# Decoder layer with 32 experts on one core: order of the experts by token count, routing on the unnormalised residual, and a last block of its own

## The reference

```
x = LN(alpha*x + mixer(x));  x = LN(alpha*x + MemCrossAttn(x, mem))
logits = x @ router_w + router_b          # 32 experts
top_val, top_idx = top_k(logits, 4);  gate = softmax(top_val)
for each chosen expert e:  h = clamped_swiglu(x @ w_gate[e] + b_gate[e], x @ w_up[e] + b_up[e])
                           y += gate * (h @ w_down[e] + b_down[e])
x = LN(alpha*x + y)
```

## Time and profile before

| | us |
|---|---|
| median of 3 runs | 1252.56 (1250.12 to 1252.93) |
| time of the profiled execution | 1252.49 |
| span of the profiled execution | 1250.4 |
| TensorE busy | 1089.8 (87%), 7535 instructions |
| VectorE busy | 317.5 (25%) |
| ScalarE busy | 189.5 (15%) |
| GpSimd busy | 35.7 (3%) |
| moved | 446.56 MB, mean 357 GB/s |

### The profile page before, as it was taken

How to read it: one execution, slowest core, us unless ns; L and a number is a source line. 1 busy time by engine, 2 the same in 40 slices (tenths; PEclk the granted TensorE clock), 3 DMA queues, 4 the chain that set the end, 5 groups by cost and what they waited for, 6 DMA issues and landing times.

```text
span 1250.4 us, 19511 instructions
## 1 busy us (share of the span) xinstructions
PE 1089.8 (87%) x7535; PEld 493.7 (39%) x7536; DVE 317.5 (25%) x973; ACT 189.5 (15%) x433; POOL 35.7 (3%) x38
## 2 busy tenths in 40 slices
PE   8999999999899999999966789776699797967885
PEld 6777874965433333333312223222233232322321
DVE  1757433213322222222211122111122221211123
ACT  1231331121111111111100011100011111100111
POOL 0110010100100000000000000000000000000001
PEclk9999999999999999999988799878799898987988
DMA  9733140557899989999999999999999999999995
GB/s 363 275 138 135 68 157 20 202 221 301 347 429 429 429 345 403 408 401 409 428 428 429 429 428 429 430 429 428 428 428 428 428 429 428 429 430 429 428 428 234
DMA packets 43687, 446.56 MB, mean 357 GB/s; under 512 B 6912, under 2 KB 7376, under 8 KB 19088
## 3 DMA queue, kind: packets, MB, share of 16 engines
q1 hardware_dynamic: 39616, 442.43, 84.5%
q10 hardware_dynamic: 4048, 3.81, 1.0%
HBM read 445.18 MB, written 1.05 MB: 357 GB/s over the span
## 4 chain that ended last, share of the span: by engine, by line
PE 60%; DMA 25%; DVE 5%; issue 3%; another core or an unknown queue 2%; DVEq 2%; SPq 1%; POOL 0%; POOLq 0%; ACT 0%; ACTq 0%
DMA main<-in_exp_w_up_dram 24%; PE bank L1318 23%; PE bank L1359 10%; PE bank L882 8%; PE bank L872 6%; PE bank L1255 2%; PE bank L1346 2%; PE bank L1122 2%; DVEq L1807 1%; DVE kst L1813 1%; DVE main L1810 1%; DVE main L1800 1%; PE bank L931 1%; DMA main<-in_w_in_dram 1%
## 5 line engine op out<-in xcount | busy, mean ns | idle before, releaser
L1318 PE MATMUL bank<-main 128*32 128x512 f32 x3008 | 392.0, 676 | 122.2 <-DMA main<-in_exp_w_up_dram 117.7
L1318 PEld LDWEIGHTS bank<-main 128*32 128x32 f32 x3008 | 113.3, 122 | 393.8 <-issue 360.1
L1359 PE MATMUL bank<-main,kst 128*32 128x512 f32 x1504 | 180.8, 598 | 16.9 <-DVE kst L1813 16.9
L1800 DVE TENSOR_TENSOR main<-bank,main 128x256 f32<-128x256 f32 x94 | 39.6, 421 | 590.9 <-PE bank L1346 590.9
L882 PE MATMUL bank<-main 128*128 128x512 f32 x256 | 111.8, 593 | 0.3 <-ACT main L693 0.3
L815 ACT ACTIVATE main<-bank 128x512 f32<-128x512 f32 x47 | 28.1, 598 | 479.2 <-PE bank L1318 479.2
L1297 PE MATMUL bank<-main 64*128 64x512 f32 x384 | 95.4, 615 | 0.7 <-ACT main L823 0.7
L872 PE MATMUL bank<-main 128*128 128x256 f32 x352 | 77.8, 380 | 0.0
L1359 PEld LDWEIGHTS bank<-main,kst 128*32 128x32 f32 x1504 | 39.3, 109 | 90.1 <-issue 64.1
L882 PEld LDWEIGHTS bank<-main 128*128 128x128 f32 x256 | 48.2, 190 | 56.7 <-issue 56.5
L872 PEld LDWEIGHTS bank<-main 128*128 128x128 f32 x352 | 66.5, 190 | 10.1 <-issue 1.1
(11 more groups left out here) (252 smaller groups left out, 707.0 us busy)
## 6 DMA issues: line engine op xcount, KB each, us to landing
main<-in_exp_w_gate_dram SPq DMA_DIRECT2D x64, 2048.0 KB, 30.2
main<-in_exp_w_up_dram SPq DMA_DIRECT2D x64, 2048.0 KB, 34.7
main<-in_exp_w_down_dram SPq DMA_DIRECT2D x64, 2048.0 KB, 36.7
...
```

What stands on the lines that cost most here:

```text
L1318: last = pe.matmul(gu_bank[at:at + CAP, :], xg_chunk(k), weights(role, k, f), start=(k == 0), stop=(k == KC - 1))
L1359: last = pe.matmul(y_bank[at:at + CAP, :], hT[:, j, f, :], weights(role, j, h), start=(f == 0 and pair == 0), stop=(f == 1 and pair == 1))
L1800: return tt(dst, gT[:, :, w, :, :], b.unsqueeze(3).broadcast_to([P, 4, 2, CAP]), ALU.add)
```

## The change

1. **Order of the experts.** Experts 0 and 1 stay first. The other 30 are ranked by token count on the chip (VectorE compares keys of 64 x count minus the expert's number), and a fixed table (`rank_at_position`) takes lightest but one, heaviest, next lightest, next heaviest and so on; the very lightest comes last. SP reads the expert's number for a position from the table (one more `value_load` an expert), TensorE goes by positions. With the counts above the blocks by position are 1, 1, 1, 3, and then 1 and 2 in turn through position 29: positions 4 to 29 alternate 1 and 2, positions 30 and 31 have one block each.
2. **Router on the residual.** The router's weights are multiplied by the norm's gain ahead of time, and mean and bias are folded in (unit `rw`). TensorE transposes the raw residual and multiplies it; VectorE scales the logits by the reciprocal root (`choose`). `xa_wo` is loaded as two halves of columns, and the units run `wo0`, `wo2`, `wo1`, `wo3` with the transposes between. `keep_warm` is gone. Token block 1 is normalised by ScalarE, its gain and bias are applied half by GpSimd and half by VectorE, and the first gather waits for both (`ln_ready` 5). Two of the four products that begin the result sums (`begin_sum`) stand behind the first gather.
3. **Tables.** `bT` moves to the cross attention. The counts are taken twice, as a column and as a row; `block_counts` has five products and `block_table` two.
4. **First transfers.** G0 and U0 of expert 0 take the slots of `xa_wq`'s halves and are released after `xq3`; D0 of expert 1 is released with G1 and U1.
5. **Last block.** It has code of its own on TensorE, ScalarE and VectorE. The scatter of the block before and the gates' transposes stand between the two halves of gate and up; gather, selection and gathered transposes are left out. The last D1 transfer is two transfers, each with its own semaphore.
6. **Last norm.** ScalarE sums and squares token block 1 with its accumulator; VectorE does all the rest; GpSimd only computes the two roots.

The diff, cut to its core (drains and blank lines left out, indentation shortened):

```diff
+def rank_at_position():
+    heavy, light = list(range(FIRST_EXPERTS, 16)), list(range(16, N_EXPERTS))
+    last = light.pop()
+    order = list(range(FIRST_EXPERTS))
+    while heavy or light:
+if light:
+    order.append(light.pop())
+if heavy:
+    order.append(heavy.pop(0))
+    return np.array(order + [last])
...
+    tie = np.where(e < FIRST_EXPERTS, 1e6 * (FIRST_EXPERTS - e), 0.0) - e
+    out[:, K_RANK + R_KEY:K_RANK + R_KEY + N_EXPERTS] = tie
+    out[0:N_EXPERTS, K_RANK + R_KEYCOL] = tie
...
-ROLE_SLOT = [(N_ATT + r) % SLOTS for r in range(SLOTS)]
+ROLE_FOLLOWS = [13, 14, 11, 12, 15, 16]
+ROLE_RELEASES = [13, 13, 15, 15, 16, 17]
+ROLE_SLOT = [i % SLOTS for i in ROLE_FOLLOWS]
...
     sp.wait_ge(mix_ready, 4)
     load_role(G0, 1, odd=True)
+    load_first(G0)
+    load_first(U0)
     sp.wait_ge(unit_filled, UNIT_AT["xs3"] + 1)
     load_role(U0, 1, odd=True)
-    for role in (G0, U0, G1, U1):
-        load_first(role)
+    load_first(G1)
+    load_first(U1)
     sp.wait_ge(unit_filled, UNIT_AT["oT3"] + 1)
     load_role(G1, 1, odd=True)
     load_role(U1, 1, odd=True)
+    load_role(D0, 1, odd=True)
     load_first(D0)
     load_first(D1)
-    sp.wait_ge(unit_filled, UNIT_AT["router"] + 1)
-    load_role(D0, 1, odd=True)
-    sp.wait_ge(ln_ready, 4)
+    sp.wait_ge(ln_ready, 5)
     load_role(D1, 1, odd=True)
     sp.wait_ge(tab_ready, 1)
...
+    def load_last_down(e):
+        w = d["exp_w_down"][0].rearrange("e (h p i j) n -> e h p i (j n)", h=2, i=2, j=2)
+        at = weights_at(D1, True)
+        for i in range(2):
+            cols = slice(at + i * SLOT_COLS // 2, at + (i + 1) * SLOT_COLS // 2)
+            sp.dma_start(main[:, cols], w[bass.ds(e, 1), 1, :, i, :].rearrange("e p n -> p (e n)")).then_inc(last_down[i], 16)
...
+    def load_expert(p, ahead, odd, last=False):
+        done = blocks_through(p, ahead - 2)
+        e = sp.value_load(itab[0:1, bass.ds(p + (T_ORDER + ahead), 1)], min_val=0, max_val=N_EXPERTS - 1)
         sp.wait_ge(gu0_used, done)
-        load_role(G0, e, odd, ahead)
-        load_role(U0, e, odd, ahead)
...
+    load_expert(N_EXPERTS - 4, 2, odd=False)
+    load_expert(N_EXPERTS - 4, 3, odd=True, last=True)
...
+    pool.wait_ge(scaled_x, 1)
+    pool.tensor_tensor(x3[:, 1, 0:HALF], x3[:, 1, 0:HALF], ln_g[:, 0:HALF], ALU.mult)
+    pool.drain()
+    pool.tensor_tensor(x3[:, 1, 0:HALF], x3[:, 1, 0:HALF], ln_b[:, 0:HALF], ALU.add).then_inc(ln_ready, 1)
...
+    act.wait_ge(offset_in, 1)
+    for h in range(2):
+        part = x3[:, 1, h * HALF:(h + 1) * HALF]
+        act.activation(part, part, ACT.Identity, scale=rstd_fin[1], bias=offset).then_inc(scaled_x, 1)
...
+        act.wait_ge(scat_done, 3 + h)
+        act.activation(x3[:, 1, h * HALF:(h + 1) * HALF], acc[1][h][:, :], ACT.Copy,
+                       accum_out=sums_fin[:, h:h + 1]).then_inc(sum_done, 1)
+    act.wait_ge(mean_ready, 1)
+    for h in range(2):
+        act.activation(x3[:, 1, h * HALF:(h + 1) * HALF], acc[1][h][:, :], ACT.Square, bias=offset,
+                       accum_out=sums_fin[:, h:h + 1]).then_inc(square_done, 1)
...
-    for i in range(4):
-        if i == 3:
-            pe.wait_ge(ln_applied, 3)
-            tokens_T("x2T", 0, x3)
-            tokens_T("x2T", 1, x3)
-        token_major(f"wo{i}", oT, i // 2, through(15, 16), (i % 2) * HALF, ((0, "oT2"), (6, "oT3")))
...
-    def keep_warm(products):
...
+    arrived(15)
+    ps = begin("wo0")
+    need("oT2")
+    wo_steps(ps, 0, range(0, 6))
+    need("oT3")
+    wo_steps(ps, 0, range(6, 8)).then_inc(unit_filled, 1)
+    wo_steps(begin("wo2"), 2, range(0, 8)).then_inc(unit_filled, 1)
+    need("wo0")
+    tokens_T("x2T", 0, x3)
+    used_up(1, "wo2")
+    arrived(16)
+    wo_steps(begin("wo1"), 1, range(0, 8)).then_inc(unit_filled, 1)
+    need("wo2")
     tokens_T("x2T", 2, x3)
+    bank_wo3 = begin("wo3")
+    wo_steps(bank_wo3, 3, range(0, 4))
+    need("wo1")
+    tokens_T("x2T", 1, x3)
+    wo_steps(bank_wo3, 3, range(4, 8)).then_inc(unit_filled, 1)
+    def route(ps, b, steps):
+        for k in steps:
+            last = pe.matmul(ps[:, 0:N_EXPERTS], x2T[b][:, k, :], router_w3[:, k, :], start=(k == 0), stop=(k == KC - 1))
+        return last
+    def begin_sum(i):
+        pe.matmul(begin(f"acc{i}")[:, :], alpha_eye, x3[:, i // 2, (i % 2) * HALF:(i % 2 + 1) * HALF],
+                  start=True, stop=False).then_inc(unit_filled, 1)
+    need("rw", "x2T1")
+    route(begin("rt0"), 0, range(0, 8)).then_inc(unit_filled, 1)
+    used_up(1, "wo3")
+    need("wo3")
     tokens_T("x2T", 3, x3)
-    keep_warm(6)
-    route_block(1, ((0, "x2T2"), (4, "x2T3"))).then_inc(unit_filled, 1)
+    ps = begin("rt1")
+    need("x2T2")
+    route(ps, 1, range(0, 4))
+    pe.wait_ge(x2T3_first, 1)
+    route(ps, 1, range(4, 6))
+    need("x2T3")
+    route(ps, 1, range(6, 8)).then_inc(unit_filled, 1)
     pe.wait_ge(alpha_ready, 1)
-    for i in range(4):
-        ps = warm_bank if i == 0 else begin(f"acc{i}")
-        pe.wait_ge(ln_ready, 3 if i < 2 else 4)
-        pe.matmul(ps[:, :], alpha_eye, x3[:, i // 2, (i % 2) * HALF:(i % 2 + 1) * HALF],
-                  start=True, stop=False).then_inc(unit_filled, 1)
-    pe.wait_ge(route_ready, 1)
+    pe.wait_ge(ln_ready, 3)
+    begin_sum(0)
+    pe.wait_ge(chosen, 1)
     ps = begin("pos")
     pe.matmul(ps[:, 0:32], strict, M[:, 0:32], start=True, stop=True)
-    pe.matmul(ps[:, 32:64], strict, M[:, 32:64], start=True, stop=False)
-    pe.matmul(ps[:, 32:64], ones, M[:, 0:32], start=False, stop=True)
+    pe.matmul(ps[:, 32:64], ones, M[:, 0:32], start=True, stop=False)
+    pe.wait_ge(chosen, 2)
+    pe.matmul(ps[:, 32:64], strict, M[:, 32:64], start=False, stop=True)
     pe.matmul(ps[0:32, 64:65], M[:, 0:32], ones[:, 0:1], start=True, stop=False)
-    pe.matmul(ps[0:32, 64:65], M[:, 32:64], ones[:, 0:1], start=False, stop=True).then_inc(unit_filled, 1)
+    pe.matmul(ps[0:32, 64:65], M[:, 32:64], ones[:, 0:1], start=False, stop=True)
+    pe.matmul(ps[0:32, 96:128], ones[:, 0:32], M[:, 0:32], start=True, stop=False)
+    pe.matmul(ps[0:32, 96:128], ones[:, 0:32], M[:, 32:64], start=False, stop=True).then_inc(unit_filled, 1)
+    begin_sum(1)
...
+    pe.wait_ge(ln_ready, 5)
     gather(begin("xg0")).then_inc(unit_filled, 1)
+    begin_sum(2)
+    begin_sum(3)
...
+        if last_block:
+            pe.wait_ge(y_copied, n + 1)
+            pe.wait_ge(gselT_ready, n + 1)
+            scatter(0)
+            scatter(1)
+            next_gates()
...
+                if last_block and role == D1:
+                    pe.wait_ge(last_down[pair], 16)
...
+    def choose(b):
+        top = top8[:, 8 * b:8 * b + 8]
+        stt(l3[:, b, :], filled(f"rt{b}")[:, 0:N_EXPERTS], rstd_fin[b], rb, ALU.mult, ALU.add).then_inc(dve_emptied, 1)
+        if b == 1:
+            stt(offset, mv_fin[1][:, 0:1], -1.0, rstd_fin[1], ALU.mult, ALU.mult).then_inc(offset_in, 1)
+        dve.max(top, l3[:, b, :])
+        dve.memset(top[:, TOP_K:8], NEG)
+        dve.match_replace(M3[:, b, :], top, l3[:, b, :], NEG)
+        ts(M3[:, b, :], M3[:, b, :], NEG, None, ALU.is_equal).then_inc(chosen, 1)
+    residual("wo0", 0, 0, bn_pair[0])
+    residual("wo2", 1, 0, bn_pair[1])
+    residual("wo1", 0, 1, bn_pair[0])
+    spread_of(0)
+    dve.wait_ge(ld_ln, 64)
+    dve.wait_ge(var_out, 7)
+    dve.wait_ge(unit_filled, UNIT_AT["x2T1"] + 1)
+    stt(x3[:, 0, :], x3[:, 0, :], mv_fin[0][:, 0:1], ln_g, ALU.subtract, ALU.mult)
+    stt(x3[:, 0, :], x3[:, 0, :], rstd_fin[0], ln_b, ALU.mult, ALU.add).then_inc(ln_ready, 1)
+    residual("wo3", 1, 1, bn_pair[1])
+    spread_of(1)
+    choose(0)
+    dve.wait_ge(var_out, 8)
+    choose(1)
...
+    upper_half = slice(HALF, D_MODEL)
+    dve.wait_ge(scaled_x, 2)
+    tt(x3[:, 1, upper_half], x3[:, 1, upper_half], ln_g[:, upper_half], ALU.mult)
+    tt(x3[:, 1, upper_half], x3[:, 1, upper_half], ln_b[:, upper_half], ALU.add).then_inc(ln_ready, 1)
...
+    stt(keys, counts_ps[0:32, 96:128], 64.0, key_row, ALU.mult, ALU.add)
...
+    ts(keys, keys, own_key, None, ALU.is_gt)
...
+    dve.reduce_sum(rank, keys, AX_X)
...
+    stt(at_rank, rank_at[:, 0:32], rank, iota[0:32, 0:32], ALU.is_equal, ALU.mult)
+    ts(at_position, rank_at, rank, None, ALU.is_equal)
...
+    def centred(b, h, minus_mean):
+        x, g, _ = halves(b, h)
+        stt(x, acc[b][h][:, :], minus_mean, g, ALU.add, ALU.mult)
+    def scaled(b, h):
+        x, _, shift = halves(b, h)
+        stt(x, x, rstd_fin[b], shift, ALU.mult, ALU.add).then_inc(out_ready, 1)
+    for h in range(2):
+        dve.wait_ge(scat_done, h + 1)
+        dve.bn_stats(bn_pair[0][:, h, :], acc[0][h][:, :])
+    spread_of(0)
+    ts(mv_fin[0][:, 0:1], mv_fin[0][:, 0:1], -1.0, None, ALU.mult)
+    dve.wait_ge(ld_ln, 96)
+    centred(0, 0, mv_fin[0][:, 0:1])
+    dve.wait_ge(sum_done, 2)
+    tt(offset, sums_fin[:, 0:1], sums_fin[:, 1:2], ALU.add)
+    ts(offset, offset, -1.0 / D_MODEL, None, ALU.mult).then_inc(mean_ready, 1)
```

(20 more changed lines are left out.)

433 lines of the change are left out of this document (240 added, 193 removed).

## The result

The changed kernel takes 1238.73 us (median of 4 runs, 1236.18 to 1238.83) against 1251.61 (1250.12 to 1252.93) before, a ratio of 0.989 (0.9879 to 0.9904): 12.9 us faster. Forecast were 1237.3 (1233.5 to 1242.0).

A forecast was written before the change was run, and what follows sets the result against it. The stream of expert weights was taken to bound the kernel, every microsecond of DMA idleness after 336 counting. Terms -12.9 - 2.3 - 0.1 + 0.1 = -15.2 took 1252.5 to 1237.3 us, range 1233.5 to 1242.

The forecast's parts named there:

- Order, -12.9: Expert weight stream: alternating light and heavy experts removes all 13.2 us of stops, less 0.3 at position 5; -13.5 to -10.
- The one microsecond in hand at position 5: Position 5's G0 may start once position 3's third block frees its buffer: data at 424.5, stream ready at 425.5.
- Start of the stream, -2.3: Front, from `wo3` to the table: first transfer behind the table issued at 333.4 instead of 335.72; -4.5 to +0.5.
- the case "lost": Front: clock falls before the gather, up to 3.3 us more there, block 0 starts at 327.8, issue at 334.2.
- VectorE beside GpSimd: Front: two VectorE passes run beside GpSimd's two and wait 0.9 us, included in the gather's start at 320.4.
- Last block, -0.1: Last block: second half -1.4, gates' transposes -0.3, idle ahead of the down products +1.6; together -1.7 to +4.
- Last norm, +0.1: Closing norm: VectorE's path takes 9.2 us against 9.1 before; -0.8 to +1.0.
- The order that gains nothing: Rival, whole stream: stops turn up elsewhere because some other limit holds the stream; 1250 us, chance 0.03.
- the slower rate: Rival, whole stream: rate falls as neighbouring transfers read experts far apart in memory; 1265 us at 415 GB/s, chance 0.03.
- The stop did not move to position 5: Rival, behind the three-block expert: the stop moves to position 5 and neighbours, three to four us back; 1241, chance 0.12.
- Routing did not gain more: Rival, front: clock holds, VectorE's small operations come faster, block 0 starts at 323; 1234 us, chance 0.10.
- The clock is low where it now matters: Rival: +1.6 for the last block's delayed half, 1.9 in down products and scatters, +0.8 at the start; 1241.5, chance 0.12.

The follow-up runs named there:

- the control: The changed kernel run once more with no edit, as base for the other runs: 1237.32 us, ratio 0.9883 to the kernel before.

## Why the prediction was right, point by point

*What bounds it.* Right. The account by the stream closes for the changed kernel as well: issue 333.4, 1.6 until data flows, 884 of data and 0.5 of stops make 1219.5, and the trace's data end at about 1219.3, forecast 1219.

*Order, -12.9.* Right in mechanism and size. The second half's start moved by 14.89, of which 2.34 are the earlier issue, so the order has 12.55; undone alone it costs 12.7. The one microsecond in hand at position 5 was enough, since its G0 was issued at 419.59, forecast 415 to 423, without a gap in the data. The added `value_load` can be read at position 2: from the end of the table's last cast to SP's issue it is 1.86 us (331.52 to 333.38) where it was 1.22 (334.50 to 335.72). The heavy experts in a row show the reverse of it, 26 us.

*Start of the stream, -2.3.* Right at 333.38, forecast 333.4, but the closeness is luck: that was the middle of two cases and neither happened cleanly, and nine profiles with this front have the issue anywhere from 333.03 to 335.12. The gather began at 320.17, forecast 320.4. Then the clock was low, as in the case "lost", and block 0 began at 326.40: from the gather to it 6.23 us, where the two cases had 4.1 and 7.4. From its first step to the issue it took 6.98 us instead of 7.9. That the early releases buy nothing held too.

*VectorE beside GpSimd.* VectorE's first pass took 1.80 us beside GpSimd's 1.26 and the second 0.69 alone; the forecast had 0.9 us of waiting, and it was 1.11. The rule of the Trainium skill, "GPSIMD Engine Reference", section 1, on two SBUF inputs agrees here again.

*Last block, -0.1: the mis-sized term, +2.25.* Two of its steps failed. The second half was to fall from 5.06 to 3.64 "without the idleness", and took 5.34. The clock was high when it began, but fell at 1209.5, 1.1 us in, behind a wait that scatter and transposes had filled up to its last 2.17 us:

```profile
1209.00:1210.00 1.00, 1.00 (x15) 0.34 (x8) 0.00 (x0) 0.00 (x0) 0.00 (x0) 0.75 1.00 426
1210.00:1211.00 1.00, 1.00 (x12) 0.36 (x7) 0.00 (x0) 0.00 (x0) 0.00 (x0) 0.50 0.96 410
```

What failed is the length of the wait. The forecast filled the 3.26 us that TensorE had waited for U1, but that wait stood behind a first half of 6.54 us. The two halves start 9.79 us apart in both traces (1213.48 and 1223.27 before, 1198.59 and 1208.38 now), as the weights come in; behind a first half of 5.34 the time to be filled is 4.45 us, and 2.3 us of work leave 2.17 idle instead of some 0.9. What an idle time of that size does was to be read in the kernel before: all 26 of its halves behind a wait for weights of 2.35 us or more took 5.06 to 6.54, and only the one behind 1.59 took 3.64. It is not a sharp rule, for in the changed kernel one of 26 halves behind 2.17 us or more, the one behind 3.07, took 3.64 as well. Ten profiles here have this code up to the second half; in nine it took 5.14 to 5.34, in one 3.64. So the scatter moved forward gains nothing there, while work up to the last 0.44 and 0.55 us was followed by 3.64 in both profiles that have it.

The second step that failed is the price behind it: the down products with the gates' step cost 2.06 more than before, where +1.6 less 0.3 was put. That the clock would fall behind the idle 2.7 us was right in eight of nine profiles; in two it stayed low for the whole of the products, 6.21 and 6.26, in the others they took 5.34. The Trainium skill, "TensorE: Matmul & The Clock Gate", section "HAM oscillation", has the next burst start cold behind an idle gap. The changed kernel's down products agree, with the clock at 0.50 from 1217 on; its second half does not, nor do the control's down products, which began at 1.00 at 1217.58 and lost the clock at 1218.4. The burst paid each time, but in part from within.

*Last norm, +0.1: -0.96.* The passes came as costed. What was too large are the small steps and the 0.1 put down between any two: statistics to last scaling took 8.26 instead of 9.2. From the end of the first statistics (1227.32) to the first centring (1227.98) it was 0.66 us, where aggregate, variance and sign with their gaps had been put at 1.0; the small instructions overlap in the records instead of standing 0.1 apart. The four errors, +0.35, 0, +2.35 and -1.06, make up the 1.6 between the forecast -15.2 and the -13.6 found; that the norm's error made good part of the last block's is luck.

*The rivals.* The order that gains nothing and the slower rate are out, with 428 GB/s throughout. The stop did not move to position 5. Routing did not gain more: block 0 began at 326.40, not at 323. "The clock is low where it now matters" is what happened in the last block, but not as it was told: the scatter ran at the high clock (1.99 us) and delayed nothing, and it was the half itself that took 1.7 more than forecast, which only looks like the rival's 1.6. Of its 1.9 more behind that, 0.8 came (2.06 for the 1.3 put). It did not reach 1241.5, since its +0.8 at the start did not come (the low clock cost 2.1 us between gather and block 0, not 3.3), and since the norm gave 1.0 back.
